# A Fourier branch on one core: full-width products over all tokens, against products over folded tokens with cosine and sine side by side in 64-column halves

## The chip, the core and the metric

The kernel runs on one core of a Trainium2 chip, as one launch. The metric is the device time in microseconds (us), the median of several executions. Engines are called as the profile calls them: PE multiplies matrices (PEld is its weight load), DVE, ACT and POOL work elementwise, SP issues transfers. A matrix product on PE reads a stationary operand (rows by output partitions) and streams a moving one; its result stands in `ps`, eight banks of 512 f32 per partition.

## The reference, cut to what matters

Two transformer blocks follow each other: the first has two layers of attention and feed-forward, the second two layers (l = 0, 1) in which each layer has three branches. The branch of this case is `_fourier`, a two-dimensional Fourier transform of the 256 columns `f_in`, four heads of 64, over tokens and over a head's 64 columns, real part only; its result goes through `w_fmix` and a gate.

```python
def _fourier(u):
    b, n, _ = u.shape
    ug = u.astype(jnp.float32).reshape(b, n, F_GROUPS, F_GROUP_DIM).transpose(0, 2, 1, 3)
    f = jnp.fft.fft2(ug, norm="ortho").real
    return f.transpose(0, 2, 1, 3).reshape(b, n, F_WIDTH).astype(u.dtype)
...
    f_out = (_fourier(f_in) @ w_fmix) * jax.nn.silu(f_gate)
    g_out = _spatial_gate(g_u, g_v, g_ln_g, g_ws, g_bs) * jax.nn.silu(g_gate)
```

It is computed for x (512 tokens) in both layers, and for y (the context, 256 tokens) in layer 0 alone, where the code says `self.both`. All of it is f32.

## The kernel before, in words

Everything is laid out feature by partition: a tile holds 128 features by tokens. `Layer` is one layer of the second block; its four engine programs are written by hand, in fixed order, with counters as semaphores (`T.wait_ge(e.u_out.h, ...)`); nothing is reordered by a scheduler. On PE a layer is `tensor_in` (the projections), `tensor_mix` (the stage of this case), `tensor_heads` (keys and queries, one job a token block), the joint attention, `tensor_out`.

`tensor_in` leaves `tm`, tokens by partition: six blocks of 128 tokens (four of x, two of y), 256 Fourier columns and 256 columns of the spatial gate each. `tensor_mix` then issues on PE:

- `fourier(0, a)`, a = 0 (cosine) and 1 (sine), for feature tile 0 (two heads): the transform over tokens, four products of 512 columns accumulated, and for y two of 256. ACT copies each result to `U`.
- the spatial gate's products (`wsT`): 64-wide stationaries, a pair of heads written to partitions 0 to 63 and 64 to 127 of one bank. DVE adds the bias and multiplies (`mixed`, `mix_gated`), ACT and DVE split the result into a high and a low part.
- `fourier(1, a)` for feature tile 1.
- the transform over a head's 64 columns, `dfd` (block diagonal, two heads, one matrix for the cosine part and one for the sine part), for each tile and each piece (x, y). ACT copies to `F_`.
- `w_fmix` (`wfm`), `project(0)`, `w_fmix` again, `project(1)` and on into `tensor_heads`. DVE's `gate_mix` multiplies the result of `w_fmix` with the gate `fg`.

ACT takes its work in this order (`scalar_mix`): two transfers issued, a table load, `U` for tile 0 (twice), the high parts of both spatial-gate tiles, `U` for tile 1 (twice), `F_` piece by piece. PE's products of `fourier(1, a)` wait for the `U` copy of the same bank, the first `dfd` product of a tile for both `U` copies of that tile.

## Time and profile before

| what | value |
|---|---|
| median of three runs | 2251.23 us (2251.19 to 2251.57) |
| the profiled execution's own time | 2252.77 us |
| its span, first to last instruction | 2251.5 us |
| PE busy | 2217.8 us, 99% of the span |
| DVE, ACT, POOL busy | 998.9 (44%), 832.7 (37%), 735.1 us (33%) |
| mean granted TensorE clock | 0.998 |

The profiled execution is 1.5 us (0.07%) above the median; its span is 1.3 us shorter than its own time. An f32 matrix product leaves two records of PE in the trace (counts in the trace are twice those in the order of instructions), while a f32r product leaves one. A record's duration reaches past the start of the next one, so a step's cost is read from start to start.

### The profile page before, as it was taken

The page shows a single profiled execution, that of the slowest core. Times are in us where ns is not written, and L with a number is a line of the kernel's source. Part 1 is how long each engine was busy: PE and PEld are TensorE (multiplying, and loading weights), DVE is VectorE, ACT ScalarE, POOL GpSimd, SP SyncE. Part 2 cuts the span into 40 slices and gives each one's busy share as a digit, 9 for nine tenths or more (in the row PEclk, how much of TensorE's full clock was granted, in tenths as well). Part 3 has the DMA queues.
Part 4 walks back from the last instruction along what each step waited for, and adds up shares of the span by engine and source line. Part 5 has one row for each costly group of instructions (what it writes and reads, how often), then busy time and mean ns, then how long its engine had stood idle before and what let it go on. Part 6 is the DMA issues. An engine that isn't in the chain of part 4 may idle for free.

```text
span 2251.5 us, 31279 instructions
## 1 busy us (share of the span) xinstructions
PE 2217.8 (99%) x13114; PEld 1795.1 (80%) x13114; DVE 998.9 (44%) x1519; ACT 832.7 (37%) x1291; POOL 735.1 (33%) x339
## 2 busy tenths in 40 slices
PE   9999999999999999999999999999999999999999
PEld 7778888888889888888778888887885667886677
DVE  5655555621222232223366555445204673541672
ACT  6544333233233343334453333333224432333531
POOL 3116444455432332323164444443220101332102
PEclk9999999999999999999999999999999999999999
DMA  4113444432322222122034444433110001322002
GB/s 147 40 47 112 140 141 147 152 103 94 116 84 67 67 66 75 66 73 68 30 103 144 150 147 141 134 100 122 57 65 33 1 1 38 131 75 80 1 1 75
DMA packets 54587, 193.36 MB, mean 86 GB/s; under 512 B 6832, under 2 KB 8112, under 8 KB 53552
## 3 DMA queue, kind: packets, MB, share of 16 engines
q1 hardware_dynamic: 43056, 153.72, 20.8%
q10 hardware_dynamic: 11392, 37.65, 4.4%
q8 instruction: 105, 1.72, 0.3%
q14 instruction: 34, 0.28, 0.0%
HBM read 189.24 MB, written 2.10 MB: 85 GB/s over the span
## 4 chain that ended last, share of the span: by engine, by line
PE 88%; DVE 3%; ACT 1%; issue 1%; DVEq 0%; DMA 0%; POOL 0%; POOLq 0%
PE ps L174 21%; PE ps L176 20%; PE ps L175 20%; PE ps L2523 4%; PE ps L177 3%; PE ps L179 3%; PE ps L178 3%; PE ps L2555 2%; PE ps L1052 2%; PE ps L1078 2%; PE ps L2535 2%; PE ps L1063 1%; PE ps L1919 1%; DVE dvS L1111 0%; DMA w_raw<-in_wstream 0%
## 5 line engine op out<-in xcount | busy, mean ns | idle before, releaser
L246 POOL TENSOR_TENSOR w_lo<-w_raw,w_hi 128x1024 fp32r<-128x1024 f32 x282 | 681.7, 2419 | 1390.4 <-ACT w_hi L164 1390.4
L174 PE MATMUL ps<-h_hi,w_hi 128*128 128x512 f32 x1168 | 469.9, 402 | 4.6 <-DVE w_lo L288 2.1
L164 ACT ACTIVATE w_hi<-w_raw 128x1024 fp32r<-128x1024 f32 x284 | 299.4, 1057 | 438.0 <-DMA w_raw<-in_wstream 436.7
L176 PE MATMUL ps<-h_hi,w_lo 128*128 128x512 f32 x1168 | 458.1, 392 | 0.0
L175 PE MATMUL ps<-h_lo,w_hi 128*128 128x512 f32 x1168 | 454.6, 389 | 0.0
L174 PEld LDWEIGHTS ps<-h_hi,w_hi 128*128 128x128 f32 x1168 | 219.5, 188 | 52.4 <-issue 4.0
L176 PEld LDWEIGHTS ps<-h_hi,w_lo 128*128 128x128 f32 x1168 | 219.3, 188 | 50.9
L175 PEld LDWEIGHTS ps<-h_lo,w_hi 128*128 128x128 f32 x1168 | 219.6, 188 | 45.5 <-issue 0.7
L1255 ACT ACTIVATE sq<-sq,dnm 128x768 f32<-128x768 f32 x64 | 59.4, 930 | 184.3 <-DVE dnm L1161 184.3
L177 PE MATMUL ps<-w_hi,h_hi 128*128 128x256 f32 x416 | 117.0, 281 | 3.2 <-DVE dvS L1111 3.2
L178 PE MATMUL ps<-w_lo,h_hi 128*128 128x256 f32 x416 | 115.2, 277 | 0.0
L179 PE MATMUL ps<-w_hi,h_lo 128*128 128x256 f32 x416 | 115.1, 277 | 0.0
L2523 PE MATMUL ps<-l_kT,l_qT 96*128 96x512 f32 (+1 forms) x288 | 103.0, 481 | 2.0 <-DVE l_work L2173 1.8
L2658 ACT ACTIVATE j_prob<-ps,j_nm 128x768 f32<-128x768 f32 (+1 forms) x80 | 65.1, 815 | 106.8 <-DVE j_nm L2597 106.8
L1161 DVE CUSTOM_DVE_ANT_0 sq<-ps,bias 128x768 f32<-128x768 f32 x64 | 58.8, 955 | 99.5 <-PE ps L1052 70.6
L177 PEld LDWEIGHTS ps<-w_hi,h_hi 128*128 128x128 f32 x416 | 78.2, 188 | 6.0 <-issue 4.5
L437 DVE TENSOR_TENSOR x<-ps,x 128x512 f32<-128x512 f32 x32 | 25.1, 786 | 129.8 <-PE ps L176 129.8
L178 PEld LDWEIGHTS ps<-w_lo,h_hi 128*128 128x128 f32 x416 | 78.1, 188 | 0.1
L179 PEld LDWEIGHTS ps<-w_hi,h_lo 128*128 128x128 f32 x416 | 78.2, 188 | 0.0
L2523 PEld LDWEIGHTS ps<-l_kT,l_qT 96*128 96x128 f32 x288 | 49.8, 192 | 35.0 <-issue 32.3
L2597 DVE TENSOR_REDUCE j_nm<-ps 128x1 f32<-128x768 f32 (+1 forms) x72 | 66.7, 926 | 19.4 <-PE ps L2523 18.7
L174 PE MATMUL ps<-l_m_hi,w_hi 128*128 128x512 f32 (+1 forms) x192 | 68.7, 358 | 0.8 <-DVE l_m_lo L2637 0.6
(323 smaller groups left out, 4141.0 us busy)
## 6 DMA issues: line engine op xcount, KB each, us to landing
w_raw<-in_wstream SPq DMA_DIRECT2D x283, 512.0 KB, 3.4
f0mod_rows<-in_wmod ACTq DMA_DIRECT2D x24, 512.0 KB, 4.2
f1mod_rows<-in_wmod ACTq DMA_DIRECT2D x24, 512.0 KB, 4.5
l_dft<-in_dft ACTq DMA_DIRECT2D x4, 1024.0 KB, 6.9
out<-x SPq DMA_DIRECT2D x8, 256.0 KB, 3.6
x<-in_x SPq DMA_DIRECT2D x3, 512.0 KB, 7.0
l_wuq<-in_wuq ACTq DMA_DIRECT2D x2, 768.0 KB, 6.7
dist<-in_dist ACTq DMA_DIRECT2D x1, 1152.0 KB, 6.4
```

The source lines that it names most:

```text
L164: self.A.activation(self.w_hi[:, n % RING, :], self.w_raw[:, n % RING, :], ACT.Copy).then_inc(self.w_high, 1)
L174: T.matmul(out, wh, ah, start=start, stop=False)
L175: T.matmul(out, wh, al, start=False, stop=False)
L176: return T.matmul(out, wl, ah, start=False, stop=stop)
L177: T.matmul(out, ah, wh, start=start, stop=False, **skip)
L178: T.matmul(out, ah, wl, start=False, stop=False, **skip)
L179: return T.matmul(out, al, wh, start=False, stop=stop, **skip)
L246: G.tensor_tensor(c.w_lo[:, n % RING, :], c.w_raw[:, n % RING, :], c.w_hi[:, n % RING, :].bitcast(F32), ALU.subtract).then_inc(c.w_low, 1)
L1255: A.activation(p, p, ACT.Exp, bias=self.nm[tile % 2][:, s:s + 1], scale=-1.0, accum_out=self.den[tile % 2][:, s:s + 1]).then_inc(self.expe ...
L2523: ins = T.matmul(c.flat(2 * (i % 2), lo, n), self.y.qT[:, head, self.cols(b)], self.y.kT[:, head, k0:k0 + n], start=True, stop=True)
L2597: c.V.tensor_reduce(self.nm[:, at:at + heads], scores, AX.X, ALU.max, negate=True).then_inc(e.maxed.h, 1)
L2658: c.A.activation(self.prob[i % 3][:, s * n:(s + 1) * n], c.flat(2 * (i % 2), s * n, n), ACT.Exp, bias=self.nm[:, at:at + 1], accum_out=sel ...
```

## The change

The transform over tokens uses symmetry. DVE's new `fold_tokens` adds and subtracts token blocks, right after the gate's first sums: blocks 0+2, 1+3 and 0-2, 1-3 of x, then (0+2)+(1+3) and (0+2)-(1+3); for y 4+5 and 4-5. Even output tokens that are multiples of four then need one product over 128 folded rows, those of 4i+2 another, and the odd ones two accumulated products of 256 columns. `fourier` takes a head (`hd`) in place of a cosine or sine: the stationary is one head's 64 columns of `fold`, and the products with the cosine matrix go to partitions 0 to 63, those with the sine matrix to partitions 64 to 127 of the same bank. The output tokens stand permuted. Since cosine and sine now lie in the 128 partitions, a head's transform over its columns is one product with a 128-row `dfd`, 64 outputs wide; two heads go to the two halves of a bank. `gate_mix` puts the tokens back in order by reading `ps` with a stride; for y it is an instruction of its own. The `dfd` products wait for the spatial gate tile by tile, and DVE does both tiles' `mix_gated` ahead of both low parts. The constants (`dft`, `dfc`, `dfd`) are smaller.

```diff
-        self.dft = [c.ctx(L + f"dft{a}", [P, TT, SEQ]) for a in range(2)]
-        self.dfc = [c.ctx(L + f"dfc{a}", [P, 2, CTX]) for a in range(2)]
+        self.dft = [c.ctx(L + f"dft{a}", [P, 6 * P]) for a in range(2)]
+        self.dfc = [c.ctx(L + f"dfc{a}", [P, CTX]) for a in range(2)]
+        self.fold = c.ctx(L + "fold", [P, 8, 256])
...
-        self.dfd = c.ctx(L + "dfd", [P, 2, P])
+        self.dfd = c.ctx(L + "dfd", [P, HD])
...
         V.tensor_reduce(groups(st[:, 1, 0:ng]), self.sqv[:, 0:nt], AX.X, ALU.add).then_inc(e.gate_summed.h, 1)
+        self.fold_tokens()
...
+    def fold_tokens(self):
+        V, tm, fold = self.c.V, self.tm, self.fold
+        V.tensor_tensor(fold[:, 4:6, :], tm[:, 0:2, 0:256], tm[:, 2:4, 0:256], ALU.add)
+        V.tensor_tensor(fold[:, 2:4, :], tm[:, 0:2, 0:256], tm[:, 2:4, 0:256], ALU.subtract)
+        if self.both:
+            V.tensor_tensor(fold[:, 6, :], tm[:, 4, 0:256], tm[:, 5, 0:256], ALU.add)
+            V.tensor_tensor(fold[:, 7, :], tm[:, 4, 0:256], tm[:, 5, 0:256], ALU.subtract)
+        V.drain()
+        V.tensor_tensor(fold[:, 0, :], fold[:, 4, :], fold[:, 5, :], ALU.add)
+        V.tensor_tensor(fold[:, 1, :], fold[:, 4, :], fold[:, 5, :], ALU.subtract).then_inc(self.e.folded.h, 1)
...
-        T.wait_ge(e.mix_gated.h, self.mg0 + 2)
         for ft in range(2):
+            T.wait_ge(e.mix_gated.h, self.mg0 + ft + 1)
             T.wait_ge(e.u_out.h, self.fu0 + 2 * ft + 2)
             for lo, nn in self.pieces:
-                T.matmul(c.flat((4, 6)[ft], lo, nn), self.dfd[:, 0, :], self.U[:, 0, ft, lo:lo + nn], start=True, stop=False)
-                T.matmul(c.flat((4, 6)[ft], lo, nn), self.dfd[:, 1, :], self.U[:, 1, ft, lo:lo + nn], start=False,
-                         stop=True).then_inc(e.f_done.h, 1)
+                for hd in range(2):
+                    ins = T.matmul(c.flat((4, 6)[ft], lo, nn)[HD * hd:HD * hd + HD], self.dfd[:, :],
+                                   self.U[:, hd, ft, lo:lo + nn], start=True, stop=True)
+                ins.then_inc(e.f_done.h, 1)
...
-    def fourier(self, ft, a):
-        c, T, bank, fs = self.c, self.c.T, (0, 2)[a], slice(ft * P, (ft + 1) * P)
-        for t in range(TT):
-            ins = T.matmul(c.ps[:, bank, :], self.tm[:, t, fs], self.dft[a][:, t, :], start=t == 0, stop=t == TT - 1)
+    def fourier(self, ft, hd):
+        c, T, bank = self.c, self.c.T, (0, 2)[hd]
+        fs, rows = slice(ft * P + hd * HD, ft * P + hd * HD + HD), [slice(HD * a, HD * a + HD) for a in range(2)]
+        fold, dft, dfc = self.fold, self.dft, self.dfc
+        for i in range(2):
+            for a in range(2):
+                T.matmul(c.flat(bank, i * P, P)[rows[a]], fold[:, i, fs], dft[a][:, i * P:(i + 1) * P], start=True, stop=True)
+        for t in range(2):
+            for a in range(2):
+                ins = T.matmul(c.flat(bank, 2 * P, 2 * P)[rows[a]], fold[:, 2 + t, fs],
+                               dft[a][:, (2 + 2 * t) * P:(4 + 2 * t) * P], start=t == 0, stop=t == 1)
         if self.both:
-            for t in range(2):
-                ins = T.matmul(c.ps[:, bank + 1, 0:CTX], self.tm[:, TT + t, fs], self.dfc[a][:, t, :], start=t == 0,
-                               stop=t == 1)
+            for i in range(2):
+                for a in range(2):
+                    ins = T.matmul(c.flat(bank + 1, i * P, P)[rows[a]], fold[:, 6 + i, fs], dfc[a][:, i * P:(i + 1) * P],
+                                   start=True, stop=True)
         ins.then_inc(self.e.fourier_done.h, 1)
...
             V.tensor_tensor(mixed, mixed, self.gu[:, pr, 0:nq], ALU.mult).then_inc(e.mix_gated.h, 1)
+        for pr in range(2):
+            mixed = self.mixed(pr)
             V.wait_ge(e.m_high.h, self.mh0 + pr + 1)
...
-        c.V.tensor_tensor(self.fg[:, ft, 0:nq], c.flat((0, 2)[ft], 0, nq), self.fg[:, ft, 0:nq],
-                          ALU.mult).then_inc(e.fmix_gated.h, 1)
+        place = lambda ap, spec: ap.rearrange(spec, a=2, b=2)
+        gate = place(self.fg[:, ft, 0:SEQ], "p (i b a) -> p i b a")
+        ins = c.V.tensor_tensor(gate, place(c.flat((0, 2)[ft], 0, SEQ), "p (a b i) -> p i b a"), gate, ALU.mult)
+        if self.both:
+            gate = self.fg[:, ft, SEQ:ALLT].rearrange("p (j a) -> p j a", a=2)
+            ins = c.V.tensor_tensor(gate, c.flat((1, 3)[ft], 0, CTX).rearrange("p (a j) -> p j a", a=2), gate, ALU.mult)
+        ins.then_inc(e.fmix_gated.h, 1)
```

PE's order at the start of layer 0's `tensor_mix`, the instructions of one bank before (the rows are line, operation, out<-in with the tiles' buffer numbers, stationary width by columns, semaphores waited for; a number after x repeats the row):

```order
L1919 MATMUL ps<-l_dft_127,l_tm 128x512 [waits rooted,l0_d_s1]
L1919 MATMUL ps<-l_dft_127,l_tm 128x512 x3
L1922 MATMUL ps<-l_dfc_129,l_tm 128x256 x2
L1919 MATMUL ps<-l_dft_128,l_tm 128x512 x4
L1922 MATMUL ps<-l_dfc_130,l_tm 128x256 x2
```

The same place now, one call of `fourier` (one head):

```order
L1944 MATMUL ps<-l_dft_127,l_fold 64x128 [waits tokens_folded,rooted,l0_d_s1]
L1944 MATMUL ps<-l_dft_128,l_fold 64x128
L1944 MATMUL ps<-l_dft_127,l_fold 64x128
L1944 MATMUL ps<-l_dft_128,l_fold 64x128
L1947 MATMUL ps<-l_dft_127,l_fold 64x256
L1947 MATMUL ps<-l_dft_128,l_fold 64x256
L1947 MATMUL ps<-l_dft_127,l_fold 64x256
L1947 MATMUL ps<-l_dft_128,l_fold 64x256
L1952 MATMUL ps<-l_dfc_129,l_fold 64x128
L1952 MATMUL ps<-l_dfc_130,l_fold 64x128
L1952 MATMUL ps<-l_dfc_129,l_fold 64x128
L1952 MATMUL ps<-l_dfc_130,l_fold 64x128
```

The first five rows of before fill two banks with 12 full-width instructions; a call of now fills one with 12 half-width ones, cosine (127, 129) and sine (128, 130) in turn. There are four such calls a layer, without the last four rows in layer 1.

DVE's order in layer 0's stage before, from the spatial gate to the second `gate_mix`:

```order
L1934 TENSOR_TENSOR l_sqv<-ps,l_bsb 128x768 [waits mixed,silu_out,w_used]
L1937 TENSOR_TENSOR l_sqv<-l_sqv,l_gu 128x768
L1939 TENSOR_TENSOR l_m_lo<-l_sqv,l_m_hi 128x768 [waits lm_high]
L1934 TENSOR_TENSOR l_sqv<-ps,l_bsb 128x768 [waits mixed]
L1937 TENSOR_TENSOR l_sqv<-l_sqv,l_gu 128x768
L1939 TENSOR_TENSOR l_m_lo<-l_sqv,l_m_hi 128x768 [waits lm_high]
L1952 TENSOR_TENSOR l_fg<-ps,l_fg 128x768 [waits fmix_done]
```

The same place now:

```order
L1964 TENSOR_TENSOR l_sqv<-ps,l_bsb 128x768 [waits mixed,silu_out,w_used]
L1967 TENSOR_TENSOR l_sqv<-l_sqv,l_gu 128x768
L1964 TENSOR_TENSOR l_sqv<-ps,l_bsb 128x768 [waits mixed]
L1967 TENSOR_TENSOR l_sqv<-l_sqv,l_gu 128x768
L1971 TENSOR_TENSOR l_m_lo<-l_sqv,l_m_hi 128x768 [waits lm_high] x2
L1986 TENSOR_TENSOR l_fg<-ps,l_fg 128x512 [waits fmix_done]
L1989 TENSOR_TENSOR l_fg<-ps,l_fg 128x256
```

The second tile's sum and product have moved ahead of the first tile's low part, and `gate_mix` has become two instructions in this layer (one in layer 1).

## Rows read from the trace of the kernel before

**Rows 1.** The page's first part: busy time, share of the span, instructions by engine.

```profile
PE 2217.8 (99%) x13114; PEld 1795.1 (80%) x13114; DVE 998.9 (44%) x1519; ACT 832.7 (37%) x1291; POOL 735.1 (33%) x339
```

**Rows 2.** Timeline of PE, layer 0's stage: start, length, instructions, idle before.

```profile
1689.33 3.59 PE L1919 MATMUL ps<-l_dft,l_tm 128*128 128x512 f32 x8
...
1693.63 3.60 PE L1919 MATMUL ps<-l_dft,l_tm 128*128 128x512 f32 x8
...
1698.02 2.84 PE L1891 MATMUL ps<-l_wsT,l_tm 128*64 128x128 f32 x48
1700.79 3.70 PE L1919 MATMUL ps<-l_dft,l_tm 128*128 128x512 f32 x8
...
1709.48 1.02 PE L1901 MATMUL ps<-l_U,l_dfd 128*128 128x512 f32 x2
...
1714.64 2.74 PE L1909 MATMUL ps<-l_F,l_wfm 128*128 128x512 f32 x8
...
1725.93 1.05 PE L2079 MATMUL ps<-ident,l_work 128*96 128x128 f32 x8 [0.81 <-ACT l_vS L2105]
```

**Rows 3.** Timeline of PE, layer 1's stage.

```profile
2054.70 7.03 PE L1919 MATMUL ps<-l_dft,l_tm 128*128 128x512 f32 x16
2061.66 1.97 PE L1891 MATMUL ps<-l_wsT,l_tm 128*64 128x128 f32 x32
2063.56 7.13 PE L1919 MATMUL ps<-l_dft,l_tm 128*128 128x512 f32 x16
2070.53 1.02 PE L1901 MATMUL ps<-l_U,l_dfd 128*128 128x512 f32 x2
...
2073.96 1.98 PE L1909 MATMUL ps<-l_F,l_wfm 128*128 128x512 f32 x4
```

**Rows 4.** Groups of instructions by form, 1689 to 1730: busy, mean ns.

```profile
L1919 PE MATMUL ps<-l_dft,l_tm 128*128 128x512 f32 x32 | 14.5, 595 | 0.0
...
L1922 PE MATMUL ps<-l_dfc,l_tm 128*128 128x256 f32 x16 | 4.1, 379 | 0.0
...
L1891 PE MATMUL ps<-l_wsT,l_tm 128*64 128x128 f32 x48 | 2.8, 275 | 0.0
```

**Rows 5.** Timeline of ACT, layer 0's stage.

```profile
1691.74 0.20 ACT L169 ACTIVATE hint<-ones 128x1 f32<-128x1 f32 x1
1693.83 0.81 ACT L1975 ACTIVATE l_U<-ps 128x768 f32<-128x768 f32 x1 [1.89 <-PE ps L1922]
...
1701.72 0.84 ACT L1979 ACTIVATE l_m_hi<-l_sqv 128x768 fp32r<-128x768 f32 x1 [2.78 <-DVE l_sqv L1937]
...
1711.40 0.60 ACT L1983 ACTIVATE l_F<-ps 128x512 f32<-128x512 f32 x1 [0.91 <-PE ps L1902]
```

**Rows 6.** Timeline of DVE, layer 0's stage.

```profile
1699.69 0.96 DVE L1934 TENSOR_TENSOR l_sqv<-ps,l_bsb 128x768 f32<-128x768 f32 x1 [56.27 <-PE ps L1891]
...
1719.77 0.69 DVE L2147 TENSOR_REDUCE l_small<-sq 128x8 f32<-128x512 f32 x1 [1.39 <-ACT sq L2095]
...
1721.72 0.96 DVE L1952 TENSOR_TENSOR l_fg<-ps,l_fg 128x768 f32<-128x768 f32 x1
```

**Rows 7.** Timeline of ACT, layer 1's stage.

```profile
2057.11 0.20 ACT L169 ACTIVATE hint<-ones 128x1 f32<-128x1 f32 x1
```

**Rows 8.** Line 437: ns min/median/max, in 1130 to 1240, then 1240 to 1545.

```profile
L437 DVE TENSOR_TENSOR x<-ps,x x8: 1054/1078/1095, 1134.7 to 1164.2; 128x512 f32<-128x512 f32 x8
L437 DVE TENSOR_TENSOR x<-ps,x x8: 678/688/692, 1422.5 to 1528.1; 128x512 f32<-128x512 f32 x8
```

**Rows 9.** Timeline of DVE around the place of the fold.

```profile
1604.96 0.19 DVE L1837 RECIPROCAL r_tok<-r_tok 128x6 f32<-128x6 f32 x1 [23.39 <-ACT r_tok L1796]
...
1998.68 0.18 DVE L1837 RECIPROCAL r_tok<-r_tok 128x4 f32<-128x4 f32 x1 [12.22 <-ACT r_tok L1796]
```

**Rows 10.** Busy time by stretch, engine by engine; after POOL's comes PE's granted clock.

```profile
1757.00:1760.00 3.00, 1.29 (x2) 0.64 (x3) 1.60 (x4) 2.88 (x5) 0.00 (x0) 0.85 0.00 0
1760.00:1765.00 5.00, 5.00 (x18) 3.09 (x17) 1.92 (x2) 1.82 (x3) 0.00 (x0) 0.75 0.00 0
```

More of the change, by code:

```diff
@@ L1550, in __init__ @@
                        (self.rope[:, :, :, :].rearrange("p a b n -> p (a b n)"), c.io["rope"])]
-        self.loads = [(self.dft[a][:, :, :], c.io["dft"][:, a]) for a in range(2)]
-        self.loads += [(self.dfd[:, :, :].rearrange("p a n -> p (a n)"), c.io["dfd"]),
+        self.loads = [(self.dft[a][:, :], c.io["dft"][:, a]) for a in range(2)]
+        self.loads += [(self.dfd[:, :], c.io["dfd"]),
                        (self.wfm[:, :, :].rearrange("p a n -> p (a n)"), c.io["wfmix"][l]),
@@ L1555, in __init__ @@
         if self.both:
-            self.loads += [(self.dfc[a][:, :, :], c.io["dfc"][:, a]) for a in range(2)]
+            self.loads += [(self.dfc[a][:, :], c.io["dfc"][:, a]) for a in range(2)]
         e = sems
@@ L1881, in tensor_mix @@
         T.wait_ge(c.rooted.h, self.st0 + 2)
+        T.wait_ge(e.folded.h, self.fl0 + 1)
         for a in range(2):
@@ L2770, in shape_constants, with dft @@
     slopes = np.tile(np.array(row)[None, :], (P, 1))
-    def dft(n, scale):
-        a = np.arange(n)
-        ang = 2 * np.pi * ((a[:, None] * a[None, :]) % n) / n
-        m = np.stack([np.cos(ang), np.sin(ang)]) * scale
-        return m.reshape(2, n // P, P, n).transpose(2, 0, 1, 3)
-    a = np.arange(64)
-    ang = 2 * np.pi * ((a[:, None] * a[None, :]) % 64) / 64
-    bd = np.zeros((2, P, P))
-    for g in range(2):
-        s = slice(64 * g, 64 * g + 64)
-        bd[0, s, s] = np.cos(ang) / 8.0
-        bd[1, s, s] = -np.sin(ang) / 8.0
+    def dft(n, rows, cols):
+        ang = 2 * np.pi * ((np.array(rows)[:, None] * np.array(cols)[None, :]) % n) / n
+        return np.stack([np.cos(ang), np.sin(ang)], axis=1) * n ** -0.5
+    p, i = np.arange(P), np.arange(P)
+    odd = np.concatenate([4 * i + 1, 4 * i + 3])
+    dft_x = np.concatenate([dft(SEQ, p, 4 * i), dft(SEQ, p, 4 * i + 2), dft(SEQ, p, odd), dft(SEQ, P + p, odd)], axis=2)
+    dft_y = np.concatenate([dft(CTX, p, 2 * i), dft(CTX, p, 2 * i + 1)], axis=2)
+    ang = 2 * np.pi * ((np.arange(HD)[:, None] * np.arange(HD)[None, :]) % HD) / HD
+    dfd = np.concatenate([np.cos(ang), -np.sin(ang)]) * HD ** -0.5
     half = A_ROPE // 2
```

9 lines of the change are left out of this document (5 added, 4 removed).

## The prediction, as it stood before the changed kernel ran

> **What bounds the kernel now.** The page comes first: PE is busy for 2217.8 us, 99% of the span [rows 1], so time is gained where PE has less to do, and only as far as nothing else keeps it waiting there. The timeline of PE then shows the two stages that the change touches. In layer 0 the first Fourier product starts at 1689.33 and the first `w_fmix` product at 1714.64, 25.3 us later [rows 2]; in layer 1 these are 2054.70 and 2073.96, 19.3 us [rows 3]. The reader is to see that the rows follow each other without a named wait: PE sets the pace. The first wait behind the stage is 0.81 us at 1725.93, where PE's transposes need values that ACT copies out behind a chain of DVE work [rows 2]. The timelines of ACT and DVE say what would stop PE if its work shrank [rows 5 to 7].
>
> **What PE's work costs.** A full-width f32 product of 512 columns costs 0.857 us: four stand between 2070.53 and 2073.96 [rows 3]. That is 1.67 ns a column. Of 64-wide products in alternating halves the spatial gate is the example: 24 of 128 columns take 2.77 us in layer 0 (1698.02 to 1700.79) and 16 take 1.90 us in layer 1 [rows 2, 3]. The eight more cost 0.87 us, 0.109 each. So a pair costs 0.218 us, what one full-width product of 128 columns would by 1.67 ns a column (0.214): the halves run at once. The rest, about 0.15 us, is the change between full and half width. A record reads 275 ns there [rows 4] while records start every 0.055 us.
>
> The token transform, before: two calls take 8.69 us in layer 0, twice (1689.33 to 1698.02, 1700.79 to 1709.48), and 6.96 and 6.97 us in layer 1 [rows 2, 3]. Now a call in layer 0 is four pairs of 128 columns and two of 256: 4 x 0.218 + 2 x 0.43 = 1.73 us; in layer 1 two and two, 1.29 us. Two calls: 3.5 and 2.6 us. The `dfd` stage, before: 5.16 us in layer 0 (1709.48 to 1714.64) and 3.43 in layer 1. Now half the columns in pairs: 2.6 and 1.7 us. The pairs of 256 and 512 columns are not in the trace; I take them to overlap as those of 128 do, and price the other case as a rival. The change of width happens twice a layer before (into and out of the spatial gate) and twice now (into the first call, out of the last `dfd` product): no difference.
>
> **Where PE will wait.** I run the new order through with the measured durations, t from the first Fourier product.
>
> Layer 0, PE: first calls until 1.8 and 3.6, spatial gate until 6.2, second calls until 7.95 and 9.7, `dfd` of tile 0 until 11.0. ACT is held by its transfers and table load until 1691.94, t = 2.6 [rows 5]; the first `U` copy is therefore 0.6 us later than its data, ends at 3.5, the second at 4.6: both ahead of the second calls. DVE starts on the spatial gate 1.67 us after its first product, as before (1699.69 after 1698.02 [rows 2, 6]), at 5.2, and its four instructions of 0.96 us, with the small gaps between them, end at 9.3. ACT's order puts both high parts (0.84 us each [rows 5]) ahead of the last two `U` copies: the second high part ends at 10.1, the copies (0.81 each) at 10.9 and 11.75. The `dfd` products of tile 1 wait for the last copy: PE stands from 11.0 to 11.8. They end at 13.1; with the change of width `w_fmix` starts at 13.3. Its second half needs `F_` of tile 1, which ACT has at 13.5, before PE gets there. Gain 25.3 - 13.3 = 12.0 us.
>
> Layer 1, the same with 512 in place of 768 columns: calls until 1.4 and 2.7, spatial gate until 4.45, calls until 5.75 and 7.05, `dfd` of tile 0 until 7.9. ACT is free at 2057.31, t = 2.6 [rows 7], and the first two copies (0.60 each, like the row of that size in [rows 5]) end at 3.3 and 3.9. DVE has both products at about 6.9 (0.69 us each, the second row of [rows 8] being of this size), ACT's second high part ends at 7.5 and the last copies at 8.1 and 8.75. PE stands for 0.9 us and `w_fmix` starts at 9.8. Gain 19.3 - 9.8 = 9.5 us. The moved low parts wait behind nothing that PE needs: DVE has been done with them when `gate_mix` begins.
>
> **What is added on DVE.** The folds are six instructions in layer 0 and four in layer 1, of at most 512 elements; at 0.69 us each [rows 8] that is at most 4.2 and 2.8 us. They stand where DVE then waits 23.4 and 12.2 us for ACT [rows 9], and PE reads them some 100 us later: nothing. Without that cover they would delay the gate's products, not PE's Fourier ones. The transfers are as many as before and smaller, and land long ahead: nothing.
>
> `gate_mix` reads `ps` out of order. Only the second one of a layer counts: the first has a wait of 1.39 us behind it, the second, 0.96 us at 1721.72, starts a chain that ends in PE's 0.81 us of waiting [rows 2, 6]. In layer 0 it becomes two instructions. From 768 elements (0.96) and 512 (0.69) an instruction costs 0.27 us for 256 elements and 0.15 us on top, so the split alone costs 0.15. The stride is not in the trace on this side. The nearest rows are those of line 437: with `x` addressed four elements apart (the eight in 1130 to 1240, order `residues`) 1.08 us, in sequence 0.69 [rows 8]. By that ratio the pair costs 1.08 + 0.65 = 1.73 us in place of 0.96, +0.8, and layer 1's +0.4. At the other end stand 0.15 and 0. I take the strided row, 1.2 us in all.
>
> The Trainium skill has two pages on this that disagree. VectorE: DVE Perf Modes, in its part on mode 1x, says that this mode makes no assumptions and takes strides and PSUM operands at one result a cycle; by it the term would be 0.15 us. SBUF — State Buffer, in its note on cachelines under the port swizzle, says that an access that crosses to a new line pays, with lines of 16 bytes in SBUF and 8 in PSUM; line 437's rows agree with it for SBUF, and by it the term would be that of the sum.
>
> **The sum.** 12.0 + 9.5 - 1.2 = 20.3 us. The profiled execution's own time is 2252.77, so it would be 2232.5; the median of runs is 1.5 us lower, so I predict **2231 us**.
>
> **The rivals.**
> 1. Handovers cost more. Each layer now has PE waiting in the stage, and PE's granted clock reads 0.85 and 0.75 in two stretches of 3 and 5 us at the start of the joint attention, in the first of which PE is busy for 1.29 us only [rows 10]: some 2.9 us at the lower level, 1.2 GHz, which cost about 1.5 us. One such spell more in each layer, and copies half a microsecond later, make 3.5 us: 2234.5. For it: ACT and DVE have work back to back now; against: the stage as it is shows full pace through the change of widths. TensorEngine Tiling in the Trainium skill, under Performance Considerations, warns of this: tiling makes TensorE faster but not the emptying of PSUM, which can become the bound. By the schedule above it does for 0.8 and 0.9 us.
> 2. The term of `gate_mix` is nearly nothing, and a spell of low clock goes: 1.2 us and up to 1 us better, 2229.
> 3. Long pairs don't overlap (two f32 streams of 256 or 512 columns run one after the other, as do those of 128 beside them). Then a call costs 3.5 and 2.6 us against 4.3 and 3.5, and `dfd` nothing less: 4 x (0.85 + 0.9) = 7 us less, minus 1.2: about 2245.5. Against it are the spatial gate's pairs; for it only that they are short.
> 4. The other side: alternating halves stop each other altogether, so that each record costs its full length. Layer 0 would have 64 records of 128 columns, 32 of 256 and 16 of `dfd` (half of 512), layer 1 32, 32 and 8. At 275, 379 and 595 ns [rows 4] that is 96 x 0.275 + 72 x 0.379 + 16 x 0.595 = 63 us against 39.9 now: 23 + 1 us slower, 2275. It decides from 39.9/184 = 0.217 us a record on; in the spatial gate records start every 0.055 us.
>
> **How the numbers follow.** The forecast 0.70 (its own range 2229.5 to 2233.5), rival 1 0.13, rival 2 0.10, rival 3 0.05, rival 4 0.02. The range 2227.5 to 2237 takes in the first three. Faster by over 0.2% (4.5 us, about what can be told from no change) are all but rival 4 and the lower edge of rival 3: 0.96; same 0.02; slower 0.02.
>
> **What would show it.** `w_fmix` starting about 13.3 and 9.8 us after the first Fourier product; records of the pairs starting in twos; a wait of 0.8 to 0.9 us ahead of the second tile's `dfd` products, ended by ACT's `U`; the strided `gate_mix` at 1.08 us for 512 elements and PE's wait behind it, 0.81 now, near 1.6 in layer 0. Wrong would be: a call of 3.5 us in layer 0 (rival 3), or the gain of a stage given back in the heads stage behind it.

## The result

The changed kernel takes **2228.24 us** by the median of its four first runs (2227.95 to 2230.9), the kernel before on the same chip 2251.4 (2251.19 to 2252.55): a ratio of 0.9899, 95% interval 0.9882 to 0.9916, 1.0% faster. The prediction was 2231, its range 2227.5 to 2237. Run again on another chip, the changed kernel had 2228.58 (2227.05 to 2230.38).

The first part of the page after, which answers to [rows 1]:

```profile
PE 2195.3 (98%) x13194; PEld 1787.4 (80%) x13194; DVE 1011.5 (45%) x1531; ACT 831.7 (37%) x1291; POOL 734.9 (33%) x339
```

PE's busy time fell by 22.5 us, the span from 2251.5 to 2229.6, by 21.9. PE's timeline in layer 0, which answers to [rows 2] (start, length, instructions, idle before and what ended it):

```profile
1689.53 0.66 PE L1944 MATMUL ps<-l_dft,l_fold 128*64 128x128 f32 x8
1690.02 1.03 PE L1947 MATMUL ps<-l_dft,l_fold 128*64 128x256 f32 x8
1690.88 0.61 PE L1952 MATMUL ps<-l_dfc,l_fold 128*64 128x128 f32 x8
1691.32 0.61 PE L1944 MATMUL ps<-l_dft,l_fold 128*64 128x128 f32 x8
...
1693.06 2.79 PE L1910 MATMUL ps<-l_wsT,l_tm 128*64 128x128 f32 x48
...
1699.15 1.46 PE L1921 MATMUL ps<-l_U,l_dfd 128*64 128x512 f32 x8
1701.00 1.51 PE L1921 MATMUL ps<-l_U,l_dfd 128*64 128x512 f32 x8 [0.39 <-ACT l_U L2012]
1702.44 2.85 PE L1929 MATMUL ps<-l_F,l_wfm 128*128 128x512 f32 x8
...
1713.89 1.05 PE L2116 MATMUL ps<-ident,l_work 128*96 128x128 f32 x8 [0.88 <-ACT l_vS L2142]
```

And in layer 1, against [rows 3]:

```profile
2041.58 0.66 PE L1944 MATMUL ps<-l_dft,l_fold 128*64 128x128 f32 x8
...
2050.03 1.08 PE L1921 MATMUL ps<-l_U,l_dfd 128*64 128x512 f32 x4 [0.42 <-ACT l_U L2012]
2051.04 1.98 PE L1929 MATMUL ps<-l_F,l_wfm 128*128 128x512 f32 x4
...
2060.64 1.05 PE L2116 MATMUL ps<-ident,l_work 128*96 128x128 f32 x8 [0.75 <-ACT l_vS L2142]
```

The reader is to see three things. A call in layer 0 is eight records of 128, eight of 256 and eight of 128 columns, and the second call's first product follows the first's by 1.79 us, the gate's the second call's by 1.74 (4.30 and 4.39 before). From the first Fourier product to the first of `w_fmix` it is 12.91 us (25.31 before) and 9.46 (19.26 before). And there is one new wait in each stage, ahead of the second tile's `dfd` products, ended by ACT's `U` copy. Up to the transposes behind the stage it is 24.36 us where it was 36.60, and 19.06 where it was 28.85: 12.24 and 9.79, together 22.03 us. The span fell by 21.9; the stage of the change starts 0.2 us later (1689.53 against 1689.33), so outside the two stages nothing of size was gained or lost.

DVE's and ACT's timelines there, against [rows 6] and [rows 5], say why the wait is as short as it is:

```profile
1697.62 0.96 DVE L1967 TENSOR_TENSOR l_sqv<-l_sqv,l_gu 128x768 f32<-128x768 f32 x1
...
1698.61 0.84 ACT L2016 ACTIVATE l_m_hi<-l_sqv 128x768 fp32r<-128x768 f32 x1 [1.06 <-DVE l_sqv L1967]
1699.36 1.49 ACT L2012 ACTIVATE l_U<-ps 128x768 f32<-128x768 f32 x2
```

DVE's last gated product ends at 1698.58, 9.05 us after the stage began, and the two copies end at 1700.85, at 11.3. Instructions that follow each other on ACT start 0.75 us apart, and the two copies 0.69, though each lasts 0.79 to 0.84.

DVE, against [rows 6]: `gate_mix` is now two instructions, the first with 512 elements read out of order from `ps`.

```profile
1709.62 0.69 DVE L1986 TENSOR_TENSOR l_fg<-ps,l_fg 128x512 f32<-128x512 f32 x1
1710.23 0.41 DVE L1989 TENSOR_TENSOR l_fg<-ps,l_fg 128x256 f32<-128x256 f32 x1
```

It takes 0.69 us, what 512 elements in sequence take in [rows 8], not 1.08.

### The profile page after: what moved, and what is told of

Same layout as the page of the kernel before. It is cut to its first block, busy times and chain, and to the rows that moved or that the text cites. A ratio compares the mean times of both kernels' runs of the same rounds, so it can differ in the third digit from the quotient of the medians.

```text
span 2229.6 us, 31455 instructions
## 1 busy us (share of the span) xinstructions
PE 2195.3 (98%) x13194; PEld 1787.4 (80%) x13194; DVE 1011.5 (45%) x1531; ACT 831.7 (37%) x1291; POOL 734.9 (33%) x339
## 3 DMA queue, kind: packets, MB, share of 16 engines
q8 instruction: 106, 1.74, 0.3%
## 4 chain that ended last, share of the span: by engine, by line
PE 86%; DVE 4%; ACT 1%; issue 1%; DVEq 1%; POOL 0%; ACTq 0%; POOLq 0%
PE ps L174 21%; PE ps L176 21%; PE ps L175 20%; PE ps L2560 4%; PE ps L177 3%; PE ps L179 3%; PE ps L178 3%; PE ps L2592 2%; PE ps L1052 2%; PE ps L1078 2%; PE ps L2572 2%; PE ps L1063 1%; DVE l_h_lo L1632 1%; DVE dvS L1111 0%; PE ps L2116 0%
```

## The experiments

Each is shown as an edit of the changed kernel, or of the version that its text names. They ran on three chips. The one of the fold alone, side by side alone, halves in blocks and the stride in SBUF gave 2252.19 us for the kernel before (13 runs); the one of the copies between, DVE's order back, one wait filled and the change again gave 2251.58; the one of blocks of two, DVE's order the same again, the same filled, and both waits filled gave 2251.13 (7 runs each). On the first of them the medians lie 1.2 to 1.6 us further above the change's 2228.24 than their stages and waits explain; the kernel before shows 0.8 of that too (2252.19 against 2251.4), the rest isn't explained. For each profile the stage's length, from the first Fourier product to the first `w_fmix` product, was read from PE's timeline:

```
                         median   layer 0   layer 1
before                  2251.4     25.31     19.26
the change              2228.24    12.91      9.46
fold alone              2233.03    15.15     10.77
side by side alone      2247.76    22.53     17.50
halves in blocks        2233.94    16.58      9.94
blocks of two           2228.23    12.94      9.50
stride in SBUF          2230.27    12.91      9.46
copies between          2227.88    12.30      8.98
DVE order back          2235.38    15.29     10.84
 the same again         2235.13    14.77     10.84
 and filled             2231.49    14.68     11.10
one wait filled         2226.87    12.30      8.97
both waits filled       2224.95    12.30      8.98
```

**The fold alone.** Tokens folded, but products full-width as before, with the block-diagonal `dfd` in two halves.

```diff
-            for a in range(2):
-                T.matmul(c.flat(bank, i * P, P)[rows[a]], fold[:, i, fs], dft[a][:, i * P:(i + 1) * P], start=True, stop=True)
+            T.matmul(c.flat(bank, i * P, P), fold[:, i, fs], dft[:, i * P:(i + 1) * P], start=True, stop=True)
```

> The fold alone: tokens are folded as in the change, but the stationary is full width (two heads), cosine in one bank and sine in the other as before, and the transform over a head's columns is the two accumulated products of before. Theory (what a product costs is its columns at 1.67 ns, and two 64-wide products at once cost what one 128-wide does): a call is 1024 columns in layer 0 and 768 in layer 1, 1.71 and 1.28 us, exactly what the change's paired call costs, so the whole gain of the token transform, 10.5 + 8.8 us, is the fold's, and only the dfd stage (2.6 + 1.7 us) is given back; PE waits for no U copy, since dfd is slower again. Time about 19.3 us under the kernel before, 2232; the change stands 3 to 4 us lower. Rival (side by side is what makes the token transform fast): a call costs near 3.4 us and the time is above 2240.

Measured: 2233.03 us (2231.9 to 2234.85), ratio 0.9916 (0.9901 to 0.993).

```profile
1690.15 0.61 PE L1939 MATMUL ps<-l_dft,l_fold 128*128 128x128 f32 x4
1690.59 1.03 PE L1941 MATMUL ps<-l_dft,l_fold 128*128 128x256 f32 x4
1691.46 0.61 PE L1945 MATMUL ps<-l_dfc,l_fold 128*128 128x128 f32 x4
1691.90 0.61 PE L1939 MATMUL ps<-l_dft,l_fold 128*128 128x128 f32 x4
```

A full-width call on folded tokens takes 1.75 us, the half-width pairs of the change 1.74. So the fold gives the whole of what the calls gain, 10.2 + 8.5 = 18.7 us of stage, and no wait for `U` appears in it. Against the change it is 2.2 + 1.3 = 3.6 us of stage short, in the 3 to 4 us that were expected; the medians are 4.8 apart.

**Side by side alone.** Cosine and sine in PE's columns and `dfd` over 128 rows, tokens not folded.

```diff
-        for i in range(2):
+        for t in range(TT):
             for a in range(2):
-                T.matmul(c.flat(bank, i * P, P)[rows[a]], fold[:, i, fs], dft[a][:, i * P:(i + 1) * P], start=True, stop=True)
+                ins = T.matmul(c.flat(bank, 0, SEQ)[rows[a]], self.tm[:, t, fs], self.dft[a][:, t, :], start=t == 0,
+                               stop=t == TT - 1)
```

> Side by side alone: no fold, the token transform over all four blocks of 512 columns, but one head at a time with cosine and sine in the two 64-column halves, dfd as one product over 128 rows. Theory: pairs of 512 columns overlap like those of 128, so a call costs 3.43 + 0.86 us as before, and only dfd shrinks, by 2.6 + 1.7 us: 4.3 us less, 2247. Rival 3 of the prediction (long pairs run one after the other): a call doubles to 8.6 us in layer 0 and 6.9 in layer 1, 31 us slower, 2282.

Measured: 2247.76 us (2245.11 to 2249.64, ten runs), ratio 0.9979 (0.997 to 0.9988).

```profile
1692.01 3.60 PE L1922 MATMUL ps<-l_dft,l_tm 128*64 128x512 f32 x16
...
1707.52 2.75 PE L1902 MATMUL ps<-l_U,l_dfd 128*64 128x512 f32 x16
```

Sixteen records of 512 columns in 3.60 us are what eight full-width ones take in [rows 2]: pairs of 512 columns overlap fully, and rival 3 has nothing left. The gain is 2.8 + 1.8 = 4.5 us of stage. `dfd` has 3.9 of it (2.68 us where it took 5.16, and 1.97 where it took 3.43); the rest lies around the spatial gate, where PE no longer passes between full and half width (its products take 2.62 us in place of 2.77, the calls beside it 4.30 in place of 4.39 and 4.40). The two halves of the change would make 23.2 us of stage together; it has 22.2, since only with both does PE reach `U` too early.

**Halves in blocks, and blocks of two.** A call's products in two other orders: all six of the cosine half, then all six of the sine half; and two of the one, two of the other.

```diff
-        for i in range(2):
-            for a in range(2):
+        for a in range(2):
+            for i in range(2):
```

> The change with one thing altered: in a call of the token transform all cosine products (first half of the columns) are issued first, then all sine products (second half), instead of in turn. The products and their sizes are the same. Theory (PE takes products in order, so two run at once only if neighbours in the order go to different halves): a call costs 3.45 us in layer 0 and 2.55 in layer 1, twice as much, except where the halves meet. 4 x 1.6 + 4 x 1.2 = 11 us more than the change, 2239 to 2241, and PE no longer waits for ACT's copies. Rival (PE looks ahead far enough to run both halves at once whatever the order): within 1 us of the change, 2228 to 2229.

Measured: 2233.94 us (2233.03 to 2235.48), between the two. PE's timeline in layer 0:

```profile
1688.84 0.65 PE L1944 MATMUL ps<-l_dft,l_fold 128*64 128x128 f32 x4
1689.33 1.03 PE L1946 MATMUL ps<-l_dft,l_fold 128*64 128x256 f32 x4
1690.19 0.27 PE L1950 MATMUL ps<-l_dfc,l_fold 128*64 128x128 f32 x1
1690.20 0.32 PE L1944 MATMUL ps<-l_dft,l_fold 128*64 128x128 f32 x1
1690.30 0.27 PE L1950 MATMUL ps<-l_dfc,l_fold 128*64 128x128 f32 x1
1690.36 0.27 PE L1944 MATMUL ps<-l_dft,l_fold 128*64 128x128 f32 x1
```

The program has four records of line 1950 (the cosine half's y products) ahead of the first of line 1944 of the sine half. That one starts at 1690.20, 0.01 us after the first of the four, and so ahead of the other three. A half starts its work before its turn, then, up to three records early by this row. On its own a half costs as much as both (four records of 256 columns 0.86 us, as eight do). A call takes 2.71 us where two halves one after the other would take 3.48 and the pairs take 1.74. In layer 1, where a half's block is four short and four long records, each block's end runs beside the next one's start, and the stage loses only 0.5 us. My theory that only neighbours overlap fell: the blocks cost 3.7 + 0.5 us of stage, not the whole serial time. Its successor made a new forecast.

> The changed kernel, with PE's products of the two halves in alternation by twos instead of by ones: in each call both products of 128 columns of the cosine half, both of the sine half, then the two of 256 columns of each half, then the y products. With whole calls of six products a half (the run of halves in blocks) a call in layer 0 took 2.71 us in place of 1.74, and the trace had products of the second half start while up to two of the first half's products (four records) ahead of them in the program had not started; in layer 1, where four products make a half, next to nothing was lost. My theory: each half has a short row of products of its own, two products deep, so blocks of two overlap fully: a call of 1.74 us and 2228 us as the changed kernel, within 0.5. The rival: only direct neighbours overlap, and every block of two costs one more product's length: some 0.2 to 0.4 us more per block, 2.4 us or more for a call and 2233 or above.

Measured: 2228.23 us (2227.43 to 2230.19), stage 12.94 and 9.50: blocks of two products (four records) cost nothing.

**The stride on the other side.** `gate_mix` walks `ps` in sequence and `fg` four elements apart.

```diff
-        gate = place(self.fg[:, ft, 0:SEQ], "p (i b a) -> p i b a")
-        ins = c.V.tensor_tensor(gate, place(c.flat((0, 2)[ft], 0, SEQ), "p (a b i) -> p i b a"), gate, ALU.mult)
+        gate = place(self.fg[:, ft, 0:SEQ], "p (i b a) -> p a b i")
+        ins = c.V.tensor_tensor(gate, place(c.flat((0, 2)[ft], 0, SEQ), "p (a b i) -> p a b i"), gate, ALU.mult)
```

> The change with gate_mix walking its elements in the other order: ps is read in sequence and the gate fg in SBUF is read and written four f32 apart (two apart for y). The result is the same. Theory (a stride costs DVE on the SBUF side, as in the rows of line 437 before, and not on the PSUM side, where the change's gate_mix took 0.69 and 0.41 us): the 512-element instruction takes 1.08 us in place of 0.69, the y one something between 0.41 and 0.65; PE's wait ahead of the first transposes grows by 0.4 to 0.6 us in layer 0 and 0.4 in layer 1; 0.8 to 1.0 us more than the change, 2229. Rival (line 437 was slow for another reason than its stride): 0.69 us, no more than the change.

Measured: 2230.27 us (2229.36 to 2232.02). The groups by form in its layer 0:

```profile
L1986 DVE TENSOR_TENSOR l_fg<-ps,l_fg 128x512 f32<-128x512 f32 x2 | 2.2, 1084 | 4.9 <-PE ps L1929 4.9
...
L1989 DVE TENSOR_TENSOR l_fg<-ps,l_fg 128x256 f32<-128x256 f32 x2 | 0.8, 414 | 0.0
```

and the same line of the changed kernel:

```profile
L1986 DVE TENSOR_TENSOR l_fg<-ps,l_fg 128x512 f32<-128x512 f32 x2 | 1.4, 692 | 4.9 <-PE ps L1929 4.9
```

1084 ns against 692, and PE's wait behind the stage grows from 0.88 to 1.25 us and from 0.75 to 1.15. So the waits grew by 0.8 us together, as forecast; the median is 2.0 us above the change's, and the remaining 1.2 are like those of the other runs on that chip. For the y tokens (line 1989) it makes no difference which side is out of order: `fg` two elements apart in SBUF, or `ps` read in jumps of 128 elements, 414 ns in both kernels. `fg` is both read and written with the stride of four here, as `x` is in line 437, so which of the two costs the time isn't separated.

**ACT's copies between the high parts.**

```diff
+                if ft == 1:
+                    A.wait_ge(e.mix_gated.h, self.mg0 + a + 1)
+                    A.activation(self.m_hi[:, 2 + a, 0:nq], self.mixed(a), ACT.Copy).then_inc(e.m_high.h, 1)
...
-            if ft == 0:
-                for pr in range(2):
-                    A.wait_ge(e.mix_gated.h, self.mg0 + pr + 1)
-                    A.activation(self.m_hi[:, 2 + pr, 0:nq], self.mixed(pr), ACT.Copy).then_inc(e.m_high.h, 1)
```

Both high parts stood ahead of the second tile's two `U` copies; now one stands ahead of each.

> The changed kernel, with ACT's order in the Fourier stage changed: high part of gate tile 0, first of the second tile's U copies, high part of tile 1, second U copy, where the change has both high parts ahead of both copies. In the changed kernel's profile PE stands 0.39 us in layer 0 and 0.42 us in layer 1 ahead of the second tile's dfd products, ended by ACT's U copy. My theory: these waits are what the handover costs (start to start 0.5 us a layer with the pipeline's emptying), and the last copy then ends 0.8 us sooner in each layer: both waits gone, about 1.0 us less than the changed kernel in all, that is 2227.2 us by its median so far. The rival: the next link is late instead (F copies ahead of the second w_fmix half, or the high part of tile 1 that the products of the gate's low parts wait for), and the wait only moves: within 0.3 us of the changed kernel.

Measured: 2227.88 us (2225.39 to 2228.41).

```profile
1698.38 2.75 PE L1921 MATMUL ps<-l_U,l_dfd 128*64 128x512 f32 x16
1701.06 2.85 PE L1929 MATMUL ps<-l_F,l_wfm 128*128 128x512 f32 x8
```

All sixteen `dfd` records run through, and the stages are 0.61 and 0.48 us shorter: the waits were worth 1.1 us and did not move. The median shows 0.7 of it (0.4 against the first four runs of the change), which alone would be no proof; 2227.2 was forecast.

**DVE's order as before.** The low part of gate tile 0 stands between the two gated products again.

```diff
-        for pr in range(2):
-            mixed = self.mixed(pr)
```

> The changed kernel with DVE's order as before: the low part of gate tile 0 stands again between the two gated products, where the change has both products ahead of both low parts. My theory: the low part waits for ACT's high part (0.84 us) and takes about 1 us itself, so the second gated product, ACT's second high part and with it the last U copy come later by 1 to 1.9 us in layer 0 and about 0.7 to 1.3 us in layer 1; PE's wait ahead of the second tile's dfd grows from 0.39 and 0.42 us to 1.4 or more and about 1.1. Together 1.5 to 2.5 us slower than the changed kernel: 2229.8 to 2230.8 us. The rival, that the order is idle because the U copies are late for another reason: no difference beyond 0.3 us.

Measured: 2235.38 us (2231.31 to 2237.14): right in direction, but 6.8 us, not 2. PE's timeline in layer 0:

```profile
1702.87 2.03 PE L1921 MATMUL ps<-l_U,l_dfd 128*64 128x512 f32 x8 [2.25 <-ACT l_U L2010]
1704.82 3.98 PE L1929 MATMUL ps<-l_F,l_wfm 128*128 128x512 f32 x8
```

And busy time by stretch around that wait, in the columns of [rows 10]:

```profile
1700.00:1703.00 3.00, 0.75 (x8) 0.31 (x6) 1.40 (x2) 2.52 (x4) 0.00 (x0) 1.00 0.00 0
1703.00:1708.00 5.00, 5.00 (x14) 2.29 (x14) 0.00 (x0) 1.47 (x4) 0.00 (x0) 0.66 0.01 3
```

The second row is the fall: the granted clock is 1.00 in the first stretch and 0.66 in the second. The waits are 2.25 and 1.81 us. Without a fall of the clock inside the stage (14.77 in the second profile, and 10.84) they lengthen it by 1.9 + 1.4 = 3.2 us. For the other 3.6 us the clock is what differs (0.997 and 0.998 in three of the four runs). Behind a wait with PE busy for 0.75 us of 3, the granted clock falls to the lower level, 1.2 GHz, and the eight `dfd` and eight `w_fmix` records take 1.95 and 3.8 us from start to next start, where the changed kernel's take 1.44 and 2.68: 1.6 us more. The second profile of this kernel has no fall at 1704 but one behind layer 1's wait, and both have four such falls, where the two profiles of the change have two and none. But only one of the four stands behind a wait that this edit has lengthened. The others stand behind waits that the change has as well, at 1547, 1750 and 2092 us, and one in the first 11 us; why there should be more of those isn't shown.

> The kernel with DVE's order as before once more, unaltered, as the measure for the filled one on the same chip. Its four runs were 2231.3 to 2237.1 us with clocks of 0.997 to 0.999. By my theory of the clock it again spreads over more than 3 us and lies 2.5 us or more above the filled one.

Measured: 2235.13 us (2232.37 to 2237.07), granted clock 0.997, 0.998, 0.998, 0.997 in its four runs. PE's timeline in its layer 1:

```profile
2054.43 1.08 PE L1921 MATMUL ps<-l_U,l_dfd 128*64 128x512 f32 x4 [1.81 <-ACT l_U L2010]
2055.44 3.36 PE L1929 MATMUL ps<-l_F,l_wfm 128*128 128x512 f32 x4
```

Four `w_fmix` records take 3.36 us here, 1.98 in the changed kernel. The four runs spread over 4.7 us and lie 3.6 above the filled kernel by their medians, as forecast.

**The same with the gap filled.** Eight products nobody reads, in both layers.

```diff
             T.wait_ge(e.mix_gated.h, self.mg0 + ft + 1)
+            if ft == 1:
+                for _ in range(8):
+                    T.matmul(c.flat(6, 0, P), c.ident[:, :], c.ident[:, :], start=True, stop=True)
             T.wait_ge(e.u_out.h, self.fu0 + 2 * ft + 2)
```

> The kernel with DVE's order as before, and on PE, between its wait for the second gated product and its wait for the last U copy, eight f32 products of 128 columns that nobody reads (8 x 0.214 = 1.7 us, in both layers). Without them that kernel took 2235.4 us, where its longer waits explain only some 3 us: 2.25 and about 1.8 us in the place of 0.39 and 0.42. In its profile the granted clock falls to 1.2 GHz directly behind the wait of 2.25 us, and there are four such spells of 3.4 us in place of the changed kernel's none to two. My theory: the long wait itself brings the clock down, and each spell costs 1.3 to 1.8 us. With PE kept at work in the same gap the waits' own cost stays and the spell at this place goes: 2232 to 2233 us, no low clock between 1700 and 1710, and the eight w_fmix products in 2.7 us, not 3.98. The rival: the spell has nothing to do with the wait, and the median stays at 2235 to 2236.

Measured: 2231.49 us (2230.33 to 2233.44), on the same chip as the 2235.13 above. PE's timeline in layer 0:

```profile
1698.54 2.05 PE L1920 MATMUL ps<-ident 128*128 128x128 f32 x16
1700.77 1.51 PE L1924 MATMUL ps<-l_U,l_dfd 128*64 128x512 f32 x8 [0.18 <-ACT l_U L2013]
1702.21 2.85 PE L1932 MATMUL ps<-l_F,l_wfm 128*128 128x512 f32 x8
```

No fall stands in either stage. The stage is as long as without the fill in layer 0 (14.68 against 14.77) and 0.3 us longer in layer 1 (11.10 against 10.84), and still the kernel is 3.6 us faster, more than the 2 to 3 forecast. The fill can claim only part of that by the profiles: the unfilled one has four falls of about 1.7 us each, this one has one, but of the three that are gone only one stood behind a filled wait. The other two stood behind waits that the fill doesn't touch; whether that is chance isn't shown. What is left over the changed kernel, 2.9 us against 2228.58 and 3.3 against the 2228.23 of the blocks of two on the same chip, is about the 3.4 us by which its two stages are longer.

**One wait filled, both waits filled.** To the kernel with the copies between, the same eight products are added in layer 0's heads stage, then also in layer 1's, where PE otherwise stands for 1.8 and 1.97 us ahead of the joint attention. Kernel before and change share these waits. The edit of layer 1 (that of layer 0 puts the same eight products at another place of the same loop):

```diff
+            elif j < NT + TT and not self.both and i == self.nj:
+                T.wait_ge(e.evacuated.h, self.ev0 + j + 1)
+                for _ in range(8):
+                    T.matmul(c.flat(self.turn_bank(j), 0, P), c.ident[:, :], c.ident[:, :], start=True, stop=True)
+                T.wait_ge(e.turned_q.h, self.tq0 + j - NT + 1)
```

> The kernel with the U copies between the high parts, and eight f32 products of 128 columns whose result nobody reads, put on PE in layer 0's heads stage ahead of the transposes that end it, where PE otherwise stands for 1.6 to 1.8 us just ahead of the joint attention. In the profile of the kernel before the granted clock is at its lower level for 3.4 us behind this wait, in that of the changed kernel it is not. If the lower level follows the wait, the fill (about 1.7 us of work, in time that is idle anyway) leaves the span as it is, and no spell stands at this place; in the runs of this kernel the time then varies less and lies at the lower edge of those of the kernel without it (up to 1.5 us below its median). The rival, that these spells fall where they fall: a spell may stand at this place or elsewhere, and the median is that of the kernel without the fill within 0.5 us, or above by what of the fill is not hidden.

Measured: 2226.87 us (2226.41 to 2228.08), 1.0 below the kernel without the fill, and no fall in the profile behind the filled wait. The four runs alone prove little: two read 0.999 and two 0.998, no better than without the fill, and the two ranges overlap.

> The kernel with the U copies between the high parts and layer 0's wait filled, with a second fill: eight f32 products of 128 columns that nobody reads in layer 1's heads stage, in the wait of 1.97 us for POOL behind which two profiles (of the changed kernel and of the one with the copies between) have a spell of low clock. My theory: a spell needs such a wait ahead of it; with both filled no profile or run has one at the joint attention of either layer, at most the one at 1547 us behind the wait of 2.17 us is left, the clock reads 0.999 in all runs and the median is 2225.5 to 2226.9. The rival: the spells move elsewhere, the clock still reads 0.998 in some runs and the median is 2227 to 2228.

Measured: 2224.95 us (2224.47 to 2225.76), ratio 0.9886 (0.9871 to 0.99); granted clock 1.000, 0.999, 1.000, 1.000; that is below the 2225.5 to 2226.9 of the forecast. PE's timeline ahead of layer 1's joint attention, in the changed kernel:

```profile
2085.83 1.23 PE L2116 MATMUL ps<-ident,l_work 128*96 128x128 f32 x8 [1.97 <-POOL l_work L2237]
2086.85 4.33 PE L2560 MATMUL ps<-l_kT,l_qT 96*128 96x512 f32 x8
```

and in this one:

```profile
2079.02 1.95 PE L2114 MATMUL ps<-ident 128*128 128x128 f32 x16
2081.16 1.08 PE L2123 MATMUL ps<-ident,l_work 128*96 128x128 f32 x8 [0.18 <-POOL l_work L2244]
2082.07 2.75 PE L2567 MATMUL ps<-l_kT,l_qT 96*128 96x512 f32 x8
```

The stretch behind the wait, first in the changed kernel and then in this one, in the columns of [rows 10] (granted clock 0.58 and 1.00):

```profile
2086.00:2090.00 4.00, 4.00 (x13) 2.51 (x12) 0.81 (x2) 2.60 (x3) 2.30 (x4) 0.58 0.00 0
...
2081.00:2085.00 4.00, 3.84 (x20) 2.65 (x21) 1.90 (x3) 2.70 (x4) 2.40 (x5) 1.00 0.00 0
```

This version is faster than both: 3.3 to 3.6 us less than the change, and its slowest run (2225.76) lies below the fastest of the change (2227.05). About 1.1 us are from the moved copies by the stages; for the rest the clock is what differs.

**All profiles together.** Leaving out the first 60 us and the last one, the fourteen profiles (kernel before, change, twelve edits) have 43 waits of PE of 1.79 us or more, and 20 falls of the clock. Each fall lasts 3.4 us and begins 0.2 to 1.6 us behind the end of one of these waits; none begins behind a shorter one. The five waits that were filled have none. Of the waits that all kernels share, 5 of 6 have a fall in the two profiles of DVE's order as before, 13 of 33 in the others. So about one such wait in two has a fall, which costs about 1.7 us (1.6 where it could be read in the stage); which one has it changes from run to run.

**The change again.**

> The changed kernel once more, unaltered, on the same chip as the three others, as the measure for them. 2228.2 us by its first four runs (2227.95 to 2230.9); by my theory of the clock spells 1 to 3 of them fall into an execution, each costing 1.5 to 1.7 us, so that single runs lie between 2227.5 and 2231.

Measured: 2228.58 us (2227.05 to 2230.38), clocks 1.000, 0.998, 0.999, 0.999. By clock, the eight runs of the change have 2230.4 and 2230.9 at 0.998, 2228.0 to 2228.9 at 0.999 (five) and 2227.05 at 1.000.

## Why the prediction held, step by step

**PE's work.** 1.73 and 1.29 us a call were predicted, 1.74 and 1.30 are in the trace (1.79 for the first call behind the change of width); `dfd` 2.6 and 1.7 predicted, 2.7 and 2.0 measured without the wait (in side by side alone), which holds most of the 0.2 us that were put on top for the change of width. That a pair costs what one full-width product does was read from pairs of 128 columns and holds for 256 and 512: shown by the fold alone and side by side alone.

**The new wait.** Its place and its releaser were right. Its size was not: 0.8 and 0.9 us were worked out, 0.39 and 0.42 are shown (about 0.5 from the last record's slot to the next start). Two things shortened it by about 0.2 us each. DVE's four instructions took 3.9 us and ended at 9.05, where I had 9.3; and I had put ACT's instructions end to end at their full lengths (2.46 us), while they took 2.24 from the first's start to the last's end. So the chain ended at 11.3 instead of 11.75; in layer 1 at 8.3 instead of 8.75, in the same two parts. So the stage gave 12.4 and 9.8, where 12.0 and 9.5 were predicted. That the wait is worth its length and nothing behind it catches up was shown by moving the copies.

**The mis-sized term.** `gate_mix` was to cost 1.2 us; PE's wait behind the stage grew by 0.07 in layer 0 and by nothing in layer 1. The step that failed is "I take the strided row": line 437's strided operand lies in SBUF, and `gate_mix` is out of order in `ps` alone. Even the split was priced too high: 0.15 us, where the pair takes 1.02 us from start to end and one instruction took 0.96. The stride moved to SBUF costs 392 ns an instruction and 0.4 us of waiting in each layer, as the row said; the same order in PSUM costs nothing. Of the two pages of the Trainium skill that were weighed, VectorE: DVE Perf Modes was right for the PSUM operand, and the note on cachelines in SBUF — State Buffer for the SBUF one; its 8-byte lines in PSUM do not show in a DVE read (692 ns against 688 in sequence).

**The moved low parts** were said to wait behind nothing that PE needs, and that holds; but the prediction only said that they are harmless, not what they were worth. Left as before they cost 6.8 us, the largest single effect of any line beside the fold: 3.2 of it waiting, which the stages show, and the rest by the clock, in part at places that the order doesn't touch.

**The folds** are under cover, as predicted: DVE then still waits 18.62 and 8.08 us for ACT, where it waited 23.39 and 12.22, and PE reads them 103 and 64 us later. They took 5.2 and 4.4 us, not at most 4.2 and 2.8, since one instruction of each layer is long. The trace shows what stands beside it:

```profile
1581.38 2.41 POOL L246 TENSOR_TENSOR w_lo<-w_raw,w_hi 128x1024 fp32r<-128x1024 f32 x1 [6.03 <-ACT w_hi L164]
1581.50 2.84 DVE L1854 TENSOR_TENSOR l_fold<-l_tm 128x512 f32<-128x512 f32 x1
```

POOL's instruction starts first and ends at 1583.79, the fold 0.55 us later. The same is in all twelve profiles with folds, once a layer: now line 1854 is long, now 1855, now 1860, and each time it started inside a `w_lo` of POOL and ended 0.55 us (512 elements) or 0.28 us (256) behind it. Two more folds start inside one, but within 0.03 us of its start; they take their usual 0.68 us, and POOL's instruction lasts 2.9 us in place of 2.4. So whichever is first holds up the other. Line 437's row at 1134.69 in the kernel before, which reads `ps` and one tile in SBUF, where a fold reads two, starts inside one too (1133.87 to 1136.28) and takes its usual 1.08 us. Here the hold-up costs nothing.

**The sum.** 12.24 + 9.79 = 22.0 us against 20.3: the missing 1.7 are about 1.1 of the `gate_mix` term and 0.7 of shorter waits. The median lies inside the range but below the forecast's own 2229.5 to 2233.5; rival 2 (2229, chance 0.10) is nearest. The outcome is rival 2 in its first half (the term is nothing); its second half, a spell of low clock less, is not shown for the profiled pair, as both have two falls to 1.2 GHz. The medians differ by 23.2 us, 1.2 more than the stages give. Runs of the same clock differ by 21.5 us at 0.998 (medians 2252.2 of 14 runs and 2230.6 of two), by 23.0 at 0.999 (2251.2 of ten and 2228.2 of five) and by 23.0 at 1.000 (2250.05 of three and 2227.05 of one), so three digits of the clock don't account for the remainder. By the profiles an estimate is 22.3: the span of the kernel before less its two falls of 1.7 us, 2248.1, against 2225.7 for the profile of the change that has none. Of 27 runs of the kernel before 14 read 0.998, of the eight of the change two. That fewer falls are the remainder fits, but with eight runs it is not settled, nor is why the change should have fewer.

**Rival 1** priced a wait by the clock, and its mechanism is real for long ones: behind the four waits of 2.25 and 1.81 us stand two falls, behind the new waits of about 0.4 us none in the four profiles that have them. The prediction's 2.9 us at the lower level, worth 1.5, was read too low from [rows 10]: a mean of 0.85 over 3 us and of 0.75 over 5 us, with half the clock as the lower level, give 0.9 + 2.5 = 3.4 us at that level, worth 1.7.

## What to carry to other kernels

Where PE is the bound, use the arithmetic first: folding cut a call from 2560 columns to 1024 (2048 to 768 in layer 1) and gave 18.7 of the 22 us, while placing two half-width streams side by side gave 4.5 when alone, nearly all of it in the next product. Then look at every wait of PE of some 2 us as dearer than its length (about one in two brought a fall of 1.7 us here), and shorten it by the order of the engines that feed it (which low part goes before which product, which copy between which) or, failing that, fill it. When a strided operand is priced from another row, ask first in which memory that row has its stride.

## What the hardware showed that was not expected

- Records of one half of PE's columns start ahead of records of the other half that stand before them in the program: up to three early in the run of halves in blocks. The Trainium skill says otherwise (TensorE: Matmul & The Clock Gate, on what overlaps and what doesn't): by it matmuls start and end strictly in program order. The starts at 1690.20 and 1690.30 differ from that, and the measurement decides. Whether products also end out of order isn't shown, since ends are modelled in the trace. A semaphore on the last product of one half is best not taken to speak for the other until that is tested.
- Reading and writing an SBUF operand four f32 elements apart costs DVE 392 ns in 512 elements. Reading the PSUM operand in jumps of 256 and 128 elements costs 4 ns (692 ns against 688). Two elements apart in SBUF costs nothing in 256 elements (414 ns).
- A fold on DVE (two operands in SBUF) and POOL's `w_lo` don't run side by side: of 26 folds that start inside a `w_lo`, 24 end 0.55 or 0.28 us behind it, up to 2.90 us in place of 0.68, and beside the other two `w_lo` lasts 2.9 us in place of 2.4.
- Eight products that nobody reads, in a gap of 2 us, went with kernels faster by 1 to 3.6 us, the 1.0 not beyond the spread of the runs and the 3.6 only in part explained by the filled waits. In the profiles read here the falls to 1.2 GHz stand behind PE's waits of 1.8 to 2.25 us (and in the first microseconds of two), but not behind each of them, and in other places from run to run: the wait of 2.25 us had one in the first profile and none in the second. The same page of the Trainium skill says in its part on the warm-up that the number of slow products at a kernel's start varies between runs of one kernel; here the falls in its middle vary as well.
